# Two hybrid blocks on one core: the values' projection taken 512 columns at a time instead of 256

## What is computed

```python
vn = _rmsnorm(v, g_v).reshape(bsz, L // MLP_CHUNK, MLP_CHUNK, MLP_GROUPS, MLP_GROUP_DIM)
sg = jnp.einsum('gqk,bckgd->bcqgd', w_s, vn) + jnp.swapaxes(b_s, 0, 1)[:, :, None]
y_b = _rmsnorm(u * sg.reshape(bsz, L, MLP_W) * jax.nn.silu(z_mlp), g_mlp)
out = jnp.concatenate([y_a, y_b], axis=-1) @ w_out
```

```python
q_sb, k_sb, v_sb, z_sb, q_r, k_r, v_r, z_r = jnp.split(proj, split_at, axis=-1)
oa = merge_heads(stick_breaking_attention(qa, ka, split_heads(v_sb, SB_HEADS))) * silu(z_sb)
ob = head_group_norm(chunkwise_retention(qr, kr, vr), ret_norm_gain) * silu(z_r)
y = jnp.concatenate([oa, ob], axis=-1) @ w_out
```

## Time and profile before

| | us |
|---|---|
| median of three executions | 2897.68 (2896.97 to 2900.3) |
| the profiled execution | 2896.28 |
| its span | 2894.5 |
| PE busy | 2833.1 (98%) |
| DVE busy | 1481.4 (51%) |
| ACT busy | 1008.3 (35%) |
| POOL busy | 360.2 (12%) |
| DMA, mean rate | 152 GB/s |

### The profile page before, as it was taken

The page is one execution under the profiler, slowest core; times in us unless marked ns, Lnnn a source line. Parts: engine busy times, 40 slices in busy tenths (PEclk is TensorE's granted clock), DMA queues, the critical chain, the costliest instruction groups (busy, mean ns, idle before and its releaser), DMA issues. The chain is left out here.

```text
span 2894.5 us, 36817 instructions
## 1 busy us (share of the span) xinstructions
PE 2833.1 (98%) x15014; PEld 2369.6 (82%) x15014; DVE 1481.4 (51%) x1760; ACT 1008.3 (35%) x1344; POOL 360.2 (12%) x411
## 2 busy tenths in 40 slices
PE   6999999999999999999999999899999999999999
PEld 2678888888889998888888888688888888888787
DVE  6868678755565456666652333623343344333532
ACT  7742222234334332433332322323343343222311
POOL 1011101001233313341210000100000000000000
PEclk8999999999999999999999999899999999999999
DMA  9657667654545554555555433232222222222342
GB/s 398 222 185 257 244 242 276 244 182 137 176 146 153 164 173 141 165 168 162 153 181 183 131 103 101 103 109 73 73 81 81 73 81 89 86 88 88 117 153 95
DMA packets 162135, 439.58 MB, mean 152 GB/s; under 512 B 14768, under 2 KB 59824, under 8 KB 151728
## 3 DMA queue, kind: packets, MB, share of 16 engines
q1 hardware_dynamic: 123360, 307.28, 33.5%
q0 software_dynamic: 15792, 92.99, 9.1%
q10 hardware_dynamic: 22816, 36.97, 3.7%
HBM read 398.11 MB, written 39.06 MB: 151 GB/s over the span
## 5 line engine op out<-in xcount | busy, mean ns | idle before, releaser
L1449 DVE TENSOR_TENSOR WL<-RAW,WH 128x1024 fp32r<-128x1024 f32 (+1 forms) x424 | 515.4, 1224 | 839.9 <-ACT WH L936 634.0
L397 PE MATMUL PB<-HH,WH 128*128 128x512 f32 x2048 | 822.4, 402 | 8.8 <-DVE WL L1449 5.6
L402 PE MATMUL PB<-HL,WH 128*128 128x512 f32 x2048 | 805.5, 393 | 0.0
L403 PE MATMUL PB<-HH,WL 128*128 128x512 f32 x2048 | 805.2, 393 | 0.0
L936 ACT ACTIVATE WH<-RAW 128x1024 fp32r<-128x1024 f32 (+1 forms) x424 | 432.1, 1038 | 462.8 <-PE PB L521 208.4
L397 PEld LDWEIGHTS PB<-HH,WH 128*128 128x128 f32 x2048 | 387.3, 189 | 98.7 <-issue 15.0
L403 PEld LDWEIGHTS PB<-HH,WL 128*128 128x128 f32 x2048 | 387.4, 189 | 67.6
L402 PEld LDWEIGHTS PB<-HL,WH 128*128 128x128 f32 x2048 | 387.7, 189 | 65.7 <-issue 3.4
L519 PE MATMUL PB<-WH,HH 128*128 128x512 f32 x768 | 300.1, 391 | 2.9 <-DVE evb L1449 1.5
L521 PE MATMUL PB<-WH,HL 128*128 128x512 f32 x768 | 299.6, 390 | 0.0
L520 PE MATMUL PB<-WL,HH 128*128 128x512 f32 x768 | 299.6, 390 | 0.0
(11 more groups left out here) (298 smaller groups left out, 3155.7 us busy)
## 6 DMA issues: line engine op xcount, KB each, us to landing
RAW<-in_w_in_t SPq DMA_DIRECT2D x320, 512.0 KB, 3.7
AU<-in_w_ada POOLq DMA_DIRECT2D x64, 1024.0 KB, 5.6
RAW<-in_w_out_t SPq DMA_DIRECT2D x96, 512.0 KB, 3.6
bcb<-R SPq DMA_DIRECT2D x64, 256.0 KB, 5.9
S<-so ACTq DMA_DIRECT2D x24, 384.0 KB, 2.7
ebc<-R SPq DMA_DIRECT2D x32, 256.0 KB, 6.2
SY<-evb ACTq DMA_DIRECT2D x32, 256.0 KB, 2.2
yin<-SY POOLq DMA_DIRECT2D x32, 256.0 KB, 4.0
```

Source lines behind the costliest of these rows:

```text
L397: h.matmul(banks[j], lh, m.HH[:, t, :], start=st, stop=False)
L402: h.matmul(banks[j], lh, m.HL[:, t, :], start=False, stop=False)
L403: ins = h.matmul(banks[j], ll, m.HH[:, t, :], start=False, stop=en)
L1449: return h.tensor_tensor(o, a, b, op)
```

## The change

Both blocks' values go through `o_unit` in blocks of 512 columns (eight units, four banks). `v_unit` is gone.

- First block: four blocks instead of eight; the number of units, 32, is the same. ACT copies banks 0 to 2 when their "out" event comes, then runs the background step that it had run before the block's end, then copies bank 3; it squares from `vbuf`, not from PSUM, 512 wide (16 squares in place of 32), and stores four pieces.
- Second block: the projections of two pairs go together, in the order z, z, q, k of the even p, then its heads start, then the values of both (eight units), then q, k of the odd p and its heads. Each pair's heads still start 16 units after the last. The gate's `silu` is written into Y2, where it is multiplied in place; Zr is gone, Vr holds two pairs' values.
- `retain` of an even p idles for 8 steps before it uses values; centring moves on DVE from the first step to the one that needs it.
- `o_unit` takes banks outside and tiles inside in its first unit as well (`kk in (0, 7)`), in the output stages too.
- The arrays of weights are packed in the new order, outside the program.

```diff
+AWAIT_V = (8, 0)
-    m.vbuf = at("vbuf", o, [128, 4, 256])
+    m.vbuf = at("vbuf", o, [128, 4, 512])
-    def v_unit(u, k4, banks, ready):
...
         last = kk == 7
-        for tt, k in [(tt, k) for k in range(4) for tt in range(2)] if last else \
+        for tt, k in [(tt, k) for k in range(4) for tt in range(2)] if kk in (0, 7) else \
                 [(tt, k) for tt in range(2) for k in range(4)]:
@@ tensor_program
-    for b in range(8):
-        tk = block(v_unit, 96 + 4 * b, first_h, "v", b)
-        for j in range(2):
-            drop(main, tk[j][0], ("vb", b, j))
+    for b in range(4):
+        tk = [take(main, "v", b, k) for k in range(4)]
+        for kk in range(8):
+            o_unit(96 + 8 * b + kk, kk, [x for _, x in tk], first_h, 20 + b)
+            step(bg)
+            step(bg2)
+        for k in range(4):
+            drop(main, tk[k][0], ("vb", b, k))
...
+    for pr in range(4):
+        u0 = AT_IN2 + 32 * pr
+        project(u0, 2 * pr, "z")
+        project(u0 + 4, 2 * pr + 1, "z")
+        project(u0 + 8, 2 * pr, "q")
+        project(u0 + 12, 2 * pr, "k")
+        heads(2 * pr)
+        tk = [take(main, "vr", pr, k) for k in range(4)]
+        for kk in range(8):
+            o_unit(u0 + 16 + kk, kk, [x for _, x in tk], second_h, 24 + pr)
+            step(bg)
+        for k in range(4):
+            drop(main, tk[k][0], ("vr", pr, k))
+        project(u0 + 24, 2 * pr + 1, "q")
+        project(u0 + 28, 2 * pr + 1, "k")
+        heads(2 * pr + 1)
@@ scalar_program
+    def take_v(b, k):
+        A.wait_ge(*(at("out", 20 + b, k) if k < 3 else at("used", 96 + 8 * b + 7)))
+        A.then(act(m.vbuf[:, k, :], bank("v", b, k), ACT.Copy), "vb", b, k)
+
+    for b in range(4):
+        block(96 + 8 * b, 7)
+        make(96 + 8 * b + 9)
...
+        for k in range(3):
+            take_v(b, k)
+        step(bg)
+        take_v(b, 3)
         for k in range(4):
+            A.wait_ge(*at("vb", b, k))
+            if k or b:
+                A.wait_ge(*at("v squared", b - (k == 0), (k - 1) % 4))
+            A.then(act(m.vjk, m.vbuf[:, k, :], ACT.Square, acc=m.vss[:, k * 4 + b:k * 4 + b + 1]), "v squared", b, k)
+        for j in range(4):
+            h.dma_start(m.VT[4 * b + j], m.vbuf[:, :, j * 128:(j + 1) * 128]) \
+                .then_inc(*land(s.VT[j], "VT", 4 * b + j))
...
+        units(u0 + 16, 7)
+        make(u0 + 25)
+        if pr:
+            A.wait_ge(*at("y2", 4 * pr - 1))
+        for k in range(4):
+            if k == 3:
                 step(bg)
+            A.wait_ge(*(at("out", 24 + pr, k) if k < 3 else at("used", u0 + 23)))
+            A.then(act(m.Vr[:, k, :], bank("vr", pr, k), ACT.Copy), "vr", pr, k)
@@ retain, on every engine
+        for idle in range(AWAIT_V[i]):
+            yield
```

More of the change, by code:

```diff
@@ L895, in tensor_program, with project, heads @@
     bg = deque([m2])
-    for p in range(8):
-        while len(bg) > 1:
+    def project(u0, p, name):
+        tk = [take(main, "proj", p, name, e) for e in range(2)]
+        for k4 in range(4):
+            t_unit(u0 + k4, k4, [tk[0][1], tk[1][1]], second_h)
             step(bg)
[L899 to L905, removed]
-        bg.append((stick if p < 4 else retain)(p))
-    while len(bg) > 1:
-        step(bg)
+        for e in range(2):
+            drop(main, tk[e][0], ("proj", p, name, e))
+    def heads(p):
+        drain(bg)
+        bg.append((stick if p < 4 else retain)(p))
+    for pr in range(4):
[14 more added lines that the diff above has]
+        heads(2 * pr + 1)
     def ready(t):
@@ L1182, in turn_half, with block @@
         A.then(act(m.HH[:, t, :], m.yin[L % 4], ACT.Copy, scale=m.P("g_ssd" if half == 0 else "g_mlp", t, 1)), "yh", L)
-    def block(u0):
-        for k4 in range(4):
+    def block(u0, n=4):
+        for k4 in range(n):
             make(u0 + k4 + 2)
@@ L1201, in scalar_program @@
             h.dma_start(m.ZS[2 * b + j], m.evb[j]).then_inc(*land(s.ev[j], "ZS", 2 * b + j))
-    for b in range(8):
-        block(96 + 4 * b)
+    def take_v(b, k):
[4 more added lines that the diff above has]
+        make(96 + 8 * b + 9)
+        for L in ahead(96 + 8 * b + 7, AT_OUT):
+            turn_half(L)
+        step(bg2)
         A.wait_ge(*at("dt"))
+        for j in range(4):
+            A.wait_ge(*(at("VT", 4 * b + j - 4) if b else at("ZS", 14 + j % 2)))
         if b:
-            A.wait_ge(*at("VT", 2 * b - 2))
-            A.wait_ge(*at("VT", 2 * b - 1))
-        for k in range(4):
[L1209 to L1218, removed]
+            A.wait_ge(*at("v squared", b - 1, 3))
+        for k in range(3):
+            take_v(b, k)
+        step(bg)
+        take_v(b, 3)
+        for k in range(4):
+            A.wait_ge(*at("vb", b, k))
+            if k or b:
+                A.wait_ge(*at("v squared", b - (k == 0), (k - 1) % 4))
+            A.then(act(m.vjk, m.vbuf[:, k, :], ACT.Square, acc=m.vss[:, k * 4 + b:k * 4 + b + 1]), "v squared", b, k)
+        for j in range(4):
+            h.dma_start(m.VT[4 * b + j], m.vbuf[:, :, j * 128:(j + 1) * 128]) \
+                .then_inc(*land(s.VT[j], "VT", 4 * b + j))
     for b in range(8):
@@ L1224, in scalar_program @@
             else:
[L1225 to L1226 removed]
+                for g in range(12, 16):
+                    A.wait_ge(*at("VT", g))
             A.then(act(m.ub[:, j, :], bank("u", b, j), ACT.Copy), "u", b, j)
@@ L1374, in scalar_program @@
     bg = deque([m2])
-    for p in range(8):
-        i = p % 2
-        while len(bg) > 1:
-            step(bg)
[L1379 to L1384, removed]
-                step(bg)
[L1386 to L1401, removed]
@@ L1402, in scalar_program, with units, project @@
-    while len(bg) > 1:
-        step(bg)
+    def units(u0, n):
+        for k4 in range(n):
+            make(u0 + k4 + 2)
+            for t in ahead(u0 + k4, AT_OUT2):
+                turn_output(t)
+            step(bg)
+    def project(u0, p, name):
+        units(u0, 4)
+        if p < 2:
+            for e in ("XD",), ("HL2", 15):
+                A.wait_ge(*at(*e))
+        elif name != "z":
+            A.wait_ge(*at("y2", 2 * p - 3))
+        A.wait_ge(*at("used", u0 + 3))
+        for e in range(2):
+            src = bank("proj", p, name, e)
+            if name == "z":
+                ins = act(m.Y2[:, 2 * p + e, :], src, ACT.Silu)
+            else:
+                ins = act((m.Qr if name == "q" else m.Kr)[p % 2][:, e, :], src, ACT.Copy)
+            A.then(ins, "proj", p, name, e)
@@ L1949, in stick @@
             V.wait_ge(*at("proj", p, "z", 1))
[L1950 to L1953, removed]
+            V.then(TT(m.Y2[:, hd, :], bank("av", hd), m.Y2[:, hd, :], ALU.mult), "y2", hd)
             if hh == 0:
@@ L1982, in retain @@
         yield
+        for idle in range(AWAIT_V[i]):
+            yield
+        vv = m.Vr[:, :, i * 256:(i + 1) * 256].rearrange("p k (h d) -> p k h d", h=2)
+        vm = m.vm.rearrange("p (k h) -> p k h", k=4)
+        V.wait_ge(*at("vr", p // 2, 3))
+        t = V.then(h.tensor_reduce(vm, vv, AXX, ALU.add))
+        V.wait_ge(*t)
+        t = V.then(TS(vm, vm, 1.0 / 128, None, ALU.mult))
+        V.wait_ge(*t)
+        V.then(TT(vv, vv, vm.unsqueeze(3).to_broadcast([128, 4, 2, 128]), ALU.subtract), "v centred", p)
         for hh in range(2):
@@ L2012, in vector_program @@
     for p in range(8):
-        while len(bg) > 1:
-            step(bg)
[L2015 to L2020, removed]
+        for k4 in range(16):
+            u = AT_IN2 + 16 * p + k4
+            make(u + 2)
+            for t in ahead(u, AT_OUT2):
+                turn_output(t)
+            step(bg)
+        drain(bg)
         bg.append((stick if p < 4 else retain)(p))
-    while len(bg) > 1:
-        step(bg)
     for nb in range(4):
@@ L2366, in retain @@
         yield
+        for idle in range(AWAIT_V[p % 2]):
+            yield
         for hh in range(2):
```

54 lines of the change are left out of this document (28 added, 26 removed).

## The result

The changed kernel takes 2889.06 us (median of five, 2882.38 to 2890.45), before 2898.65 (five, 2896.97 to 2904.52): ratio 0.996, 95% interval 0.9946 to 0.9974. Measured a second time (e0_after, beside a before of 2897.55) it took 2883.44 (2880.37 to 2886.84), ratio 0.9951 (0.9939 to 0.9964). It is faster by 0.4 to 0.5%, and its executions spread over some 8 us in the first set and 6.5 in the second. The profiled execution took 2885.41, its span is 2883.6, against 2894.5 before.

A forecast was written before the change was run, and what follows sets the result against it. PE, busy for 98% of the span, was taken to bound the kernel through its matmul stream. Width saved 20.1 us, hand-overs cost 5.4, other terms zero: -14.7 us, from 2897.68 to 2883.0 us, range 2876 to 2893.

The forecast's parts named there:

- The width: Values matmuls: 1536 pairs of 256 columns become single 512-column ones, 13.1 ns saved each, 20.1 us in all.
- my signs of being wrong: Wide matmuls not 226.8 ns apart, a hand-over waiting over 2 us, or the clock falling behind one.
- The hand-overs: PE's waits for all four banks in front of values blocks, eight times, costing 5.4 us in all.
- The first unit's loops: Banks outside, tiles inside in a wide block's first unit: zero, since waits for all four banks stand ahead.
- ACT behind a block of values: Squares and stores ahead of the next WH and WL: hidden with 2 us to spare, otherwise 0 to 4 us.
- The second block's order: Reordered projections of two pairs: taken as 0, bounds -0.5 and +2.5 us; up to four table loads go.
- The end: Last heads meeting the output stage: centring moved behind rotation comes before the first `decayed` either way, costing 0.
- The sum: 20.1 us saved less 5.4 us of hand-overs: 14.7 us gained, giving 2883.0 us on the median.
- That the clock falls behind hand-overs: Rival: each of five visible hand-overs brings a low-clock stretch costing 1.7 us, giving 2891.5 us; 12%.
- Nothing waits: Rival: the hand-over waits are covered or the end gives back its saving; 2877.6 us, down to 2876; 12%.
- width gives nothing: Rival: values matmuls pay their 13 ns by columns in their own place, giving 2903.1 us; 4%.
- The slower rival: ACT's background step ahead of bank 3's copy waits, PE with it; 2916.9 us if at all three v to v hand-overs; 6%.

The follow-up runs named there:

- e0_after: The changed kernel measured again without any edit, beside a before of 2897.55 us; 2883.44 us, ratio 0.9951 to the kernel before.
- e2_narrow: The changed kernel with each 512-column values matmul issued as two of 256, order, banks, copies and waits kept; 2906.12 us, ratio 1.0027 to the kernel before.
- e3_tileouter: The changed kernel with the wide blocks' first unit looping tiles outside again, as before the change; 2886.28 us, ratio 0.9954 to the kernel before.
- e1_lazy: The changed kernel with each bank's wait moved to the first matmul writing it, in values and output stages; 2878.94 us, ratio 0.9934 to the kernel before.
- e4_late: The changed kernel with ACT's squares and stores of a first-block values block moved behind the next block's first WH; 2883.17 us, ratio 0.9954.
- e7_all: The changed kernel with bank waits spread, squares behind the next WH, and both pairs' values centred at once in `retain`; 2875.33 us, ratio 0.9924.
- e6_bgfirst: The changed kernel with ACT's background step ahead of all four copies of a values block, in both blocks; 2895.16 us, ratio 0.999.

## Why the prediction was right, and where it wasn't

The measured median, 2889.06, lies in the range, 6 us above the forecast of 2883.0; the second set of five gave 2883.44. Faster was forecast, and it is. Of the 14.7 us forecast, the two sets gave 9.6 and 14.1 against their own before; that the second comes so near is partly luck, since by the measure behind unit 64 the change is worth 11.8. Point by point:

- **The width**, 20.1 us forecast. The mechanism is shown by e2_narrow: some 13 ns for each matmul. ("Whatever its width" says more than the two widths that were measured.) The term was a little too large, 19.0 us, since I took the wide distance from a stretch of the output stage without background and it is 1.3 ns longer in the v stage. The trace before had that figure: its 512-column matmuls of z_ssd and of u are 227.9 ns apart. The distance in the v stage was one of my signs of being wrong, and it came, at 1 us. The Trainium skill ("TensorE: Matmul & The Clock Gate", "Back-to-back issue gap") gives the formula by which the pair gains 2.5 ns for a matmul by itself and not for a stream with weight loads, which I left out; the streams here don't follow it, with 119.9 and 226.7 to 228.0 ns.
- **The hand-overs**, forecast 1.4, 0.1, 0 and 0.7 us in the first block, 1.6, 0, 0 and 1.6 in the second. Measured 1.48, 0, 0, 0.48, 1.64, 0, 0, 1.64: 5.2 us for 5.4. At unit 103 PE does wait, its first matmul starts 0.37 us late, but eight matmuls on only 0.03 us of that are left.
- **The first unit's loops**: nothing, as forecast, by e3_tileouter, and e1_lazy shows the reason, the waits ahead of the unit.
- **ACT behind a block of values** is the step that failed. I followed the moved squares and stores to the next WH and WL, found 2 us to spare there, and that held. I didn't follow them to SP: which loads are queued behind the RAW load that waits for a WH made later. The load of xT is, and the term that I had at nothing was 2.3 us more wait than before, and in some executions a stretch of low clock behind it, some 1.7. It explains with the shorter gain in width why the v stage gave 4.6 us where 9.2 were forecast: 2.3 + 1.7 + 768 x 1.3 ns = 1.0 make 5.0. In e0_after, without the low clock, the stage gave 6.4. ACT's order is enough to cause the wait: e2_narrow has it (2.5 us) at the old pace, and e4_late doesn't. But PE's faster pace adds to it, against what I expected of e4_late: PE comes to xT 0.8 us sooner behind the block's end, beside the 1.6 us by which the load is late.
- **The second block's order**: -8.2 us measured, -6.9 forecast; one stretch of low clock fewer than before (three in place of four) is 1.7 of it. None of ACT's table loads went, where I had up to four: there are 53 as before.
- **The end**: centring behind the rotation costs nothing, as forecast. PE's waits of 0.7 and 2.5 us there became one of 3.6, and e7_all shows that DVE's chain with the centring on it sets that one: with the centring off it, 2.6 us of the wait go.
- **The sum.** 19.0 from the width, less 5.2 at the hand-overs and 2.3 at xT, make 11.5 us; the measure behind unit 64 gave 11.8.
- **The rivals.** That the clock falls behind hand-overs didn't happen: in none of the changed kernel's two traces does a low stretch follow one of the gaps of 1.4 to 1.7 us. It did happen behind the 2.7 us one. (The longer idle stretch of which the prediction speaks is the 13.7 us in which PE stands still from 1836.4 on, before, with the granted clock at 0.50 from 1839.5 for 17.1 us.) "Nothing waits" and "width gives nothing" are excluded. The slower rival, ACT's background step waiting ahead of a copy, did not strike: at unit 111 `y` was there and ACT didn't wait for it, and in the second block, where the step does wait, only the last bank's copy stands behind it, which is next needed four units on. e6_bgfirst is that rival made real, at another place than I had put it, the stick heads' `later` in the second block, and it takes back nearly the whole gain by the medians and 5.3 us by the measure.

What stays open is why the early stage spreads over 7 us, and how much of the difference between 2889.06 and 2883.44 is due to that.

## What to carry to other kernels

Where PE is busy throughout, count its instructions: widening a matmul to the full bank saves the fixed part of one for each that goes (some 13 ns here, from 256 to 512 columns). The price is the buffering, since a block that holds all banks has to wait for the last copy of the one before; wait for each bank at its first use and write the first unit bank by bank, and most of the price is gone (7.4 of 8.4 us here). When work is put in front of a conversion on one engine, follow it through every queue that waits for that conversion, the loads queued behind it included.

## What the runs showed of the hardware

- Matmuls of 512 columns were 228.0 ns apart beside the scan's background and 226.7 without it; those of 256 columns were 119.9 in both blocks. The cause wasn't tried.
- A gap of 2.5 to 3.1 us in PE's work was followed by 3.4 us at the low clock in four of six traces (after, e1_lazy, e3_tileouter, e6_bgfirst) and not in the others (e0_after, e2_narrow); of the two gaps of 2.98 us in e6_bgfirst the first was followed by it. None of the gaps of 0.5 to 1.7 us in front of wide blocks was, in the two traces of the changed kernel. What decides isn't shown. One kernel's time moves by 1.7 us for each such stretch, which is why single traces have to be compared with those stretches taken out.
